# The second norms' scale spread ahead of the sixth piece, and the first block gates behind the first short-convolution piece

## The reference, cut to what matters

```python
# first block, its end
x = x + rms_norm(mixed, mix_post_g)
h = rms_norm(x, ffn_pre_g)                       # a second norm
gt, up = jnp.split(h @ w_gate_up, 2, axis=-1)
f = (jax.nn.silu(gt) * up) @ w_down
x = x + rms_norm(f, ffn_post_g)
# second block, its start
h = rms_norm_2(x, norm1_g)                       # a second norm again
z = h @ w_in
lru_x, lru_gate, sc_b, sc_c, sc_x = jnp.split(z, splits, axis=-1)
lru_x = causal_dwconv(lru_x, lru_conv_w) + lru_conv_b
r = sigmoid(block_diag(lru_x, wa) + ba)          # the block gates
i = sigmoid(block_diag(lru_x, wx) + bx)
...
y_sc = sc_b * causal_dwconv(sc_c * sc_x, sc_conv_w)   # the short convolution
```

## Time and profile before

| | |
|---|---|
| time before, median of 3 executions | 906.33 us (906.28 to 906.91) |
| the profiled execution, its own time | 907.11 us |
| its span, first to last instruction | 905.0 us |
| PE busy | 895.5 us, 99% |
| DVE busy | 745.6 us, 82% |
| ACT busy | 589.9 us, 65% |
| POOL busy | 38.0 us, 4% |
| mean granted TensorE clock | 0.999 |

### The profile page before, as it was taken

How to read it: one execution, slowest core, us unless ns; L and a number is a source line. 1 busy time by engine, 2 the same in 40 slices (tenths; PEclk the granted TensorE clock), 3 DMA queues, 4 the chain that set the end, 5 groups by cost and what they waited for, 6 DMA issues and landing times.

```text
span 905.0 us, 18388 instructions
## 1 busy us (share of the span) xinstructions
PE 895.5 (99%) x6629; PEld 846.7 (94%) x6629; DVE 745.6 (82%) x1387; ACT 589.9 (65%) x1020; POOL 38.0 (4%) x50
## 2 busy tenths in 40 slices
PE   9999999999999999999999999999999999999997
PEld 7999999999999999998888889989999999999886
DVE  5999898889889988889988666889979988888543
ACT  5649878798777485666666636679656756666432
POOL 1000111111110000000000000100000000000000
PEclk9999999999999999999999999999999999999999
DMA  8576578878876647447655555355447465555601
GB/s 335 179 270 228 146 196 237 243 209 242 227 202 207 210 146 251 163 141 248 204 186 185 197 187 171 123 194 188 144 137 258 148 202 183 178 180 177 232 2 46
DMA packets 48511, 172.05 MB, mean 190 GB/s; under 512 B 5668, under 2 KB 6344, under 8 KB 48328
## 3 DMA queue, kind: packets, MB, share of 16 engines
q1 hardware_dynamic: 43488, 154.74, 51.2%
q0 software_dynamic: 2880, 10.49, 6.1%
q10 hardware_dynamic: 2088, 6.08, 1.8%
HBM read 159.72 MB, written 1.09 MB: 178 GB/s over the span
## 4 chain that ended last, share of the span: by engine, by line
PE 68%; issue 24%; DVE 6%; ACT 1%; DMA 1%; POOL 1%; SPq 0%; POOLq 0%; DVEq 0%
PE A L488 10%; PE A L489 10%; PE A L490 10%; PE B L731 6%; PE A L522 4%; PE B L522 3%; PE B L812 2%; PE B L488 2%; PE B L489 2%; PE B L490 2%; PE A L524 2%; DVE w_lo L1457 2%; PE B L524 2%; PE A L812 2%; PE A L501 1%
## 5 line engine op out<-in xcount | busy, mean ns | idle before, releaser
L1457 DVE TENSOR_TENSOR w_lo<-raw,w_hi 128x1024 fp32r<-128x1024 f32 x249 | 301.8, 1220 | 63.5 <-ACT w_hi L965 62.4
L965 ACT ACTIVATE w_hi<-raw 128x1024 fp32r<-128x1024 f32 x249 | 259.2, 1051 | 69.9 <-PE A L813 20.6
L488 PE MATMUL A<-h,w_hi 128*128 128x256 f32 x957 | 276.0, 288 | 0.2 <-DVE sc L2120 0.2
L490 PE MATMUL A<-h,w_lo 128*128 128x256 f32 x957 | 270.7, 283 | 0.0
L489 PE MATMUL A<-h,w_hi 128*128 128x256 f32 x957 | 270.6, 283 | 0.0
L488 PEld LDWEIGHTS A<-h,w_hi 128*128 128x128 f32 x957 | 183.4, 192 | 3.3 <-issue 2.6
L489 PEld LDWEIGHTS A<-h,w_hi 128*128 128x128 f32 x957 | 183.5, 192 | 0.3
L490 PEld LDWEIGHTS A<-h,w_lo 128*128 128x128 f32 x957 | 183.3, 192 | 0.0
L488 PE MATMUL B<-h,w_hi 128*128 128x256 f32 x352 | 100.1, 284 | 0.0
L489 PE MATMUL B<-h,w_hi 128*128 128x256 f32 x352 | 99.6, 283 | 0.0
L490 PE MATMUL B<-h,w_lo 128*128 128x256 f32 x352 | 99.6, 283 | 0.0
(11 more groups left out here) (345 smaller groups left out, 1655.9 us busy)
## 6 DMA issues: line engine op xcount, KB each, us to landing
raw<-in_weights_dram SPq DMA_DIRECT2D x289, 512.0 KB, 4.4
w_lo<-raw POOLq DMA_DIRECT2D x20, 512.0 KB, 4.8
csrow<-cs_dram ACTq DMA_DIRECT2D x9, 512.0 KB, 4.8
x<-in_x_dram SPq DMA_DIRECT2D x4, 256.0 KB, 4.5
bd<-in_lru_w_dram ACTq DMA_DIRECT2D x1, 1024.0 KB, 5.5
out_dram<-m_wide SPq DMA_DIRECT2D x3, 256.0 KB, 2.1
raw<-in_weights_dram SPq DMA_DIRECT2D x2, 256.0 KB, 4.9
par<-in_params_dram SPq DMA_DIRECT2D x1, 379.0 KB, 6.6
```

Of the source, the lines that this page charges most:

```text
L488: mm(dst, wh, lo, start=first, stop=False, skip_group_check=free)
L490: return mm(dst, wl, hi, start=False, stop=last, skip_group_check=free)
L965: F(w_hi[:, s, :], raw[:, s, :], ACT.Copy).then_inc(hi_ready, 1)
L1457: V.tensor_tensor(w_lo[:, s, :], raw[:, s, :], w_hi[:, s, :].bitcast(F32), ALU.subtract).then_inc(lo_ready, 1)
```

## The change

At the first place the two transposes of `spread_scale` stand ahead of the whole piece p+5 instead of in its middle; this holds for both calls of `scaled_four`. At the second place block_gates(0) stands behind the first short-convolution piece SC0 instead of ahead of it. No instruction is added or removed on any engine, and the lists of DVE, ACT, POOL and SP are as they were.

```diff
@@ scaled_four
                 pe.wait_ge(m_scaled, norm_n // 2 - 5)
                 chunk_piece(p + 4, 0, banks[4], h_hi, h_lo, half_way=lambda: summed_squares(summed_n, norm_bank))
-                chunk_piece(p + 5, 0, banks[5], h_hi, h_lo, half_way=lambda: spread_scale(norm_n, norm_bank))
+                spread_scale(norm_n, norm_bank)
+                chunk_piece(p + 5, 0, banks[5], h_hi, h_lo)
@@ behind the second scaled_four
             chunk_piece(LRUX0 + 7, 0, LRU_BANKS[7], h_hi, h_lo)
-            block_gates(0)
             consumed = sc_copied, sc_x_used, sc_ready
             for n in range(3 * KSC):
...
                 chunk_piece(SC0 + n, 0, sc_bank(n), h_hi, h_lo)
+                if n == 0:
+                    block_gates(0)
                 if n in (1, 3, 5):
                     block_gates(n + 1)
```

## The result

The changed kernel takes 912.74 us (median of 4 executions, 911.67 to 913.61), the kernel before beside it 906.62 us (4, 906.28 to 907.36). The ratio is 1.0063, with a 95% interval of 1.0051 to 1.0075: 6.1 us slower, where 3.7 were forecast, and above the upper end of the range, 911.2 us. The sign and the mechanism are the forecast ones, and more than a third of the loss is not in the sum.

What follows compares the result with a forecast made beforehand. TensorE, busy 895.5 of 905.0 us, was taken to bound the kernel, with DVE also tight around the second place. 0.72 + 3.01 = 3.73 us on a median of 906.33 gave 910.1 us, range 908.6 to 911.2.

Steps and rivals of the forecast that it cites:

- what TensorE does with the lost time: TensorE sets the pace of the feed-forward layer; every microsecond it loses there or at the gates stays lost.
- The earlier `rs`: First spread: `rs` ready 0.78 us earlier, so DVE starts earlier; worth nothing, as TensorE waits for none of it.
- the first spread: 376 to 402 us: the transposes, 12 matmuls earlier, must wait for POOL's scale; loss 0.72 us.
- the second spread with POOL's 1.60: 580 to 594 us: POOL again needs 1.60 us for the scale, so TensorE waits 1.57; loss 1.44 us.
- the lower bound, 0.53: Second spread: the loss if POOL took 0.69 us, as with DVE idle, instead of 1.60.
- the 0.49 of the prediction's bound without a chain: Second place: the loss if no chain stood behind the gates, 1.44 - 0.67 - 0.28 us.
- the chain behind the gates: ACT's late first gates delay its weight copy, DVE's low part and block 3's convolution, then block_gates(2): all 3.01 us later.
- 1.44 + 2.88 - 0.67 - 0.64: Second place's loss: half piece, plus SC0 ahead of gates, less the old bank wait, less the time the table hides.
- the stop of 2.5 us: New wait of TensorE before block_gates(2), for the delayed convolution of block 3; forecast at 2.5 us.
- The rival without a chain: block_gates(2) does not hang on delayed ACT work: loss 0.72 + 0.49 = 1.21, 907.5 us; chance 0.10.
- the rival "the clock": TensorE's granted clock falls around the new waits: one piece at 1.2 GHz costs 2.88 more, 913.0 us; chance 0.05.
- the prediction's three signs of being wrong: The 2.5 wait missing or small; POOL taking 0.7 not 1.6 at the second place; 402 to 565 us shorter.

Runs made afterwards that it cites:

- e5: The changed kernel again, unaltered, in more rounds: 912.29 us against 907.03 for the kernel before, ratio 1.0056.
- e10: The kernel before with spread_scale ahead of the sixth piece in the first scaled_four alone: 907.61 us against 906.79.
- e2: The kernel before with the spreads' edit alone, at both places, gates as before: 908.33 us against 906.80.
- e3: The changed kernel with 19 matmuls of zeros filling the stop ahead of block_gates(2): 910.48 us against 906.80 for the kernel before.
- e8: The changed kernel with 10 matmuls of zeros half filling the stop ahead of block_gates(2): 910.61 us against 907.03 for the kernel before.
- e4: The kernel before with the gates' edit, and ACT's copy of LRUX0+13 and block 3's tap ahead of the gates, table loaded early: 906.64 us against 906.80.
- e6: The changed kernel with ACT's copy of LRUX0+13 and block 3's tap ahead of the gates, table loaded early: 908.89 us against 907.03 for the kernel before.
- e1: The kernel before with the gates' edit alone, block_gates(0) behind SC0, spreads as before: 909.45 us against 906.80.
- e7: The changed kernel with the waits at the two spreads filled by 5 and 12 matmuls of zeros: 911.29 us against 907.03 for the kernel before.

## Why the prediction was right and where it failed

**Right: what TensorE does with the lost time.** What it lost at the two places was still missing at the third mark, 3.01 us behind the second mark in e5. The earlier `rs` bought nothing that the runs can tell (e10, 0.82 us slower where 0.72 was forecast).

**Right: the first spread.** 0.72 us forecast, 0.70 to 0.75 between the marks in all seven kernels with this edit.

**Right: the second spread with POOL's 1.60.** It is 1.60 again in the changed kernel, so the lower bound, 0.53, was rightly not taken. e2 gives 0.52 for this edit with the gates where they were, the 0.49 of the prediction's bound without a chain.

**Right: the chain behind the gates.** 1.44 + 2.88 - 0.67 - 0.64 = 3.01 was measured at 3.01 (e5), 2.98 (e3), 2.99 (e8). e4 and e6 show the mechanism by taking it away: with the gates at the same place on TensorE, and on ACT the copy of LRUX0+13 and one tap moved ahead and the table loaded early, the stop of 2.5 us disappears. That the copy is the link, and not the table, is read from DVE's idle 4.65 us; no run moved the copy alone. The rival without a chain is refuted. The sum as a whole, 3.73, is what the changed kernel loses in executions in which the clock stays up: e3 lost 3.68, e8 3.58, and two of the nine executions of the changed kernel, with a mean clock of 0.999, took 910.60 and 910.89 us.

**Wrong: the clock.** The step that failed is the rival "the clock", which got a chance of 0.05, and with it the upper end of the range. The argument was that the trace before shows no fall at waits up to 0.7 us; that said nothing about 2.5. None of the prediction's three signs of being wrong came (the 2.5 is there, POOL takes 1.60, 1 to 2 has become longer, not shorter), for none of them looked at the clock. In the changed kernel's other seven executions the mean clock was 0.996 to 0.998 and the time 911.67 to 913.61 us. The mechanism stood in the list, its price there was one piece at half speed, 2.88 us; measured are 1.48 us in the profile, since the low level lasts only some 3 us, of which half is lost, and 1.68 us between the medians of the changed kernel and of e8 in the same measurement (912.29 and 910.61). e3 and e8 show the cause: with TensorE busy with zeros and everything else equally late, this loss is gone in all ten executions (910.02 to 911.11 us), while seven of nine of the changed kernel have it. The fall itself is seen in two profiles, the changed kernel's and e1's; for the other executions it is concluded from mean clock and time together.

**Not in the sum: scatter.** The first measurement's 6.1 us was 0.9 above the second's 5.3, which agrees with 3.7 + 1.5. In its profiled execution 0.95 us lay in the first loads; whether the same holds for its other three executions is not known. The kernel before was 0.29 us higher here than the 906.33 from which the forecast starts. Without the 1.48 of the clock, the first measurement would have lain at 911.3, at the upper end of the range: the clock alone took the time clearly out of it, but scatter had used up the room.

**Open:** why the clock falls in some executions of one program and not in others (by mean clock and time seven of nine with both stops, four of eight in e1, one of five in e7), whether the stop at the spread adds to it, and the 0.6 us of e1 that neither the waits nor the clock explain.

## What to carry to other kernels

Before a waiting instruction is moved later on one engine, look at what stands behind its result on the others: by the traces ACT's three sigmoids were in nobody's way, the weight copy behind them was. Where a new wait of TensorE comes out of the sum, price it twice, once as time and once as a possible fall of the clock behind it, and widen the range for it; ten or twenty matmuls on zeros in the gap are a cheap test of the second price. And compare marks inside two traces rather than their spans: that separated 0.95 us of scatter, 3.7 us of waits and 1.5 us of clock here.

## What the runs showed of the hardware

- A stop of TensorE of 2.3 us in the list of waits (2.5 between possible starts) was followed, in part of the executions, by a stretch at the lower clock: 0.61 granted in the mean of 604 to 608 us (0.50 from 605 on), matmuls 0.21 us apart instead of 0.12, back at 1.00 by 612. Behind stops of 1.4 us (e2, e6) and 1.1 us (e8) no profile shows it.
- The fall differs from one execution to the next: the same kernel gave a profile with it (the first) and one without it (e5). Whether the program changes how often it comes is open.
- ACT's first sigmoid can start 1.29 us behind the start of the table load (595.79 against 594.50 in e4), and the load itself does not wait for the gates' matmuls. In e4 a sigmoid of one column placed early took the load with it, and the first gates followed at 597.37 without idling; no run shows what e4 would be without that sigmoid.
